# Delta rule in a two-block model: ScalarE scales the query-state product, VectorE adds the rest, and ScalarE sums the squares

## The reference, cut to what matters

```python
def step(state, inp):
    u_i, w_i, qg_i, kd_i, att_i, dl_i = inp
    v_new = u_i - jnp.einsum("bhcd,bhde->bhce", w_i, state)
    o = jnp.einsum("bhcd,bhde->bhce", qg_i, state) + jnp.einsum("bhij,bhje->bhie", att_i, v_new)
    state = state * dl_i[..., None, None] + jnp.einsum("bhcd,bhce->bhde", kd_i, v_new)
    return state, o
...
o_gdn = (rmsnorm_2(o_gdn, gdn_norm_g[l]) * jax.nn.silu(z))
```

## Time and profile before

| | us |
|---|---|
| median of 3 runs (2519.55 to 2521.11) | 2519.91 |
| the profiled execution | 2520.09 |
| its span, first to last instruction | 2518.3 |
| PE busy, 99% of the span | 2481.8 |
| DVE busy, 64% | 1619.7 |
| ACT busy, 48% | 1205.7 |

### The profile page before, as it was taken

The page is one execution under the profiler, slowest core; times in us unless marked ns, Lnnn a source line. Parts: engine busy times, 40 slices in busy tenths (PEclk is TensorE's granted clock), DMA queues, the critical chain, the costliest instruction groups (busy, mean ns, idle before and its releaser), DMA issues.

```text
span 2518.3 us, 37877 instructions
## 1 busy us (share of the span) xinstructions
PE 2481.8 (99%) x15440; PEld 2070.1 (82%) x15440; DVE 1619.7 (64%) x2585; ACT 1205.7 (48%) x2030; POOL 75.2 (3%) x114
## 2 busy tenths in 40 slices
PE   9999999999999999999999999999999999999998
PEld 7999888888877777878999888777776788888887
DVE  6888348866764554357887257766877655677733
ACT  6556244666555455245555246544333454444421
POOL 0111000000000000000110000000000000000000
PEclk9999999999999999999999999999999999999999
DMA  5776332222222222333775323211111112333232
GB/s 173 175 179 154 108 100 92 77 76 75 84 68 68 76 66 77 91 92 101 176 177 151 98 93 101 76 41 37 44 43 52 59 55 88 94 99 101 88 100 72
DMA packets 80525, 237.82 MB, mean 94 GB/s; under 512 B 8928, under 2 KB 10976, under 8 KB 80352
## 3 DMA queue, kind: packets, MB, share of 16 engines
q1 hardware_dynamic: 68832, 213.56, 27.0%
q0 software_dynamic: 10080, 18.35, 4.8%
q10 hardware_dynamic: 1440, 3.49, 0.4%
HBM read 233.27 MB, written 2.10 MB: 93 GB/s over the span
## 4 chain that ended last, share of the span: by engine, by line
PE 92%; DVE 5%; DMA 2%; ACT 1%; issue 1%; SPq 0%; ACTq 0%; DVEq 0%
PE bank L2208 22%; PE bank L2210 21%; PE bank L2209 21%; PE bank L2222 4%; PE bank L2224 4%; PE bank L2223 4%; PE bank L2441 2%; PE bank L2366 1%; PE bank L2280 1%; PE bank L2374 1%; DMA raw<-in_w2u 1%; PE bank L2360 1%; PE bank L2537 1%; PE bank L2347 1%; PE bank L2258 1%
## 5 line engine op out<-in xcount | busy, mean ns | idle before, releaser
L2208 PE MATMUL bank<-uR,hl 128*128 128x512 f32 x1684 | 685.4, 407 | 5.3 <-DVE uR L2954 2.8
L2943 DVE TENSOR_TENSOR hl<-raw,hl 128x1024 fp32r<-128x1024 f32 (+2 forms) x325 | 386.0, 1191 | 453.9 <-ACT hl L2586 452.8
L2210 PE MATMUL bank<-uR,hl 128*128 128x512 f32 x1684 | 658.3, 391 | 0.0
L2209 PE MATMUL bank<-uR,hl 128*128 128x512 f32 x1684 | 657.7, 391 | 0.0
L2586 ACT CAST hl<-raw 128x1024 fp32r<-128x1024 f32 (+2 forms) x325 | 329.8, 1020 | 207.2 <-PE bank L2210 196.1
L2208 PEld LDWEIGHTS bank<-uR,hl 128*128 128x128 f32 x1684 | 316.8, 188 | 94.8 <-issue 24.8
L2209 PEld LDWEIGHTS bank<-uR,hl 128*128 128x128 f32 x1684 | 317.1, 188 | 67.6 <-issue 7.2
L2210 PEld LDWEIGHTS bank<-uR,hl 128*128 128x128 f32 x1684 | 316.5, 188 | 67.7
L2937 DVE TENSOR_TENSOR hl<-raw,hl 128x1024 fp32r<-128x1024 f32 (+1 forms) x142 | 150.8, 1076 | 32.4 <-ACT hl L2582 29.4
L2222 PE MATMUL bank<-sum,hl 128*128 128x256 f32 x560 | 159.3, 284 | 2.5 <-DVE fA L3082 2.5
L2223 PE MATMUL bank<-sum,hl 128*128 128x256 f32 x560 | 158.7, 283 | 0.0
(11 more groups left out here) (499 smaller groups left out, 4385.5 us busy)
## 6 DMA issues: line engine op xcount, KB each, us to landing
raw<-in_win SPq DMA_DIRECT2D x147, 512.0 KB, 3.5
raw<-in_w SPq DMA_DIRECT2D x44, 512.0 KB, 3.5
raw<-in_w1u SPq DMA_DIRECT2D x54, 256.0 KB, 3.0
raw<-in_w2u SPq DMA_DIRECT2D x51, 256.0 KB, 3.1
raw<-in_w1g SPq DMA_DIRECT2D x22, 512.0 KB, 4.5
raw<-in_w2g SPq DMA_DIRECT2D x22, 512.0 KB, 4.3
raw<-in_w1d SPq DMA_DIRECT2D x16, 512.0 KB, 3.6
raw<-in_wssd SPq DMA_DIRECT2D x16, 512.0 KB, 3.5
```

The costliest lines, as they stand in the source:

```text
L2208: e.matmul(s.bank[:, :], h[:, 0, w], hi, start=s.first and q == 0, stop=False)
L2209: e.matmul(s.bank[:, :], h[:, 0, w], lo, start=False, stop=False)
L2210: i = e.matmul(s.bank[:, :], h[:, 1, w], hi, start=False, stop=s.last and q == n - 1)
L2943: e.tensor_tensor(h[:, 1, w], x[:, w], h[:, 0, w].bitcast(F), ALU.subtract).then_inc(*sig("dve_split.lo", s, i))
```

## The change

In `scan_s` ACT now writes `o`: it multiplies the query-state product by `exp(G)` out of PSUM (for chunk 0, where there is no state yet, it copies the attention product). DVE then makes one addition of the attention product to `o` where it made a copy and a multiply-add. In `gdn_norm` ACT squares `o` in eight pieces of 128 columns with the sum of each taken along; the two sums on DVE are gone. The planner's table gets the new figures, and because of them the plan between pair 0 and the sparse attention comes out in another order. The bank of the products is free after DVE's addition, as before.

```diff
@@ COSTS
-               ("DVE", 0.6, "dve_gdn.o")],
-    "gdn_norm": [("ACT", 1.25), ("DVE", 1.0, "dve_gdn.sum"), ("ACT Ln", 0.45), ("DVE", 1.4, "dve_gdn.on")],
+               ("ACT", 0.3, "act_gdn.o"), ("DVE", 0.3, "dve_gdn.o")],
+    "gdn_norm": [("ACT", 2.3, "act_gdn.sq", 1), ("ACT Ln", 0.45), ("DVE", 1.4, "dve_gdn.on")],
@@ scalar_program
+        def scan_s(s):
+            c, to = s.c, tcol(s.c % 4)
+            go.wait_ge(*on("pe_gdn.o", s))
+            go.wait_ge(*on("act_gdn.dl", s.cols))
+            if c % 4 == 0:
+                after(*s.o[c // 4].after)
+            if c:
+                x = e.mul(s.o[c // 4][:, to], s.bo[:, 0:128], of_pair(geg, s.p)[:, c, :])
+            else:
+                x = e.copy(s.o[0][:, to], s.bo[:, 128:256])
+            x.then_inc(*sig("act_gdn.o", s))
+
         def gdn_norm(s):
             rs = ors[:, 0:8]
             for n in range(2):
                 after(*s.o[n].t, *s.qs[n].after)
-                activate(s.qs[n][:, :], s.o[n][:, :], ACT.Square, scale=DSC).then_inc(*sig("act_gdn.sq", s, n))
-            go.wait_ge(*on("dve_gdn.sum", s))
+                for t in range(T4):
+                    x = activate(s.qs[n][:, tcol(t)], s.o[n][:, tcol(t)], ACT.Square, scale=DSC,
+                                 accum_out=rs[:, 4 * n + t:4 * n + t + 1])
+                x.then_inc(*sig("act_gdn.sq", s, n))
+            go.wait_ge(*on("act_gdn.sq", s, 1))
@@ vector_program
-            go.wait_ge(*on("pe_gdn.o", s))
-            if c % 4 == 0:
-                after(*s.o[c // 4].after)
             if c:
-                e.tensor_copy(s.o[c // 4][:, to], s.bo[:, 128:256]).then_inc(*sig("dve_gdn.o2", s))
-                go.wait_ge(*on("dve_gdn.o2", s))
-                x = e.scalar_tensor_tensor(out=s.o[c // 4][:, to], in0=s.bo[:, 0:128], scalar=of_pair(geg, s.p)[:, c, :],
-                                           in1=s.o[c // 4][:, to], op0=ALU.mult, op1=ALU.add)
-            else:
-                x = e.tensor_copy(s.o[0][:, to], s.bo[:, 128:256])
-            x.then_inc(*sig("dve_gdn.o", s))
+                go.wait_ge(*on("act_gdn.o", s))
+                e.tensor_tensor(s.o[c // 4][:, to], s.o[c // 4][:, to], s.bo[:, 128:256], ALU.add).then_inc(*sig("dve_gdn.o", s))
@@ vector_program gdn_norm
-            for n in range(2):
-                go.wait_ge(*on("act_gdn.sq", s, n))
-                x = e.reduce_sum(rs[:, 4 * n:4 * n + 4], v3(s.qs[n]), AX.X)
-            x.then_inc(*sig("dve_gdn.sum", s))
```

More of the change, by code:

```diff
@@ L1883, in gdn_scan @@
                 x.release(("dve_gdn.state", s2, i))
-            bo.release(("dve_gdn.o", s2))
+            bo.release(("dve_gdn.o" if c else "act_gdn.o", s2))
             before = s2
@@ L1897, in gdn_out @@
         for q in qs:
-            q.release(("dve_gdn.sum", s))
+            q.release(("act_gdn.sq", s, 1))
         yield from until(lambda: zg[hs[1]] is not None)
@@ L2902, in scalar_program @@
               "turn_v": turn_v, "pv_turn": pv_turn, "pv_mul": pv_mul, "att_front": att_front, "narrow": narrow,
-              "narrow_turn": narrow_turn, "gdn_decay": gdn_decay, "gdn_seed_turn": gdn_seed_turn, "gdn_level": gdn_level,
+              "narrow_turn": narrow_turn, "scan_s": scan_s, "gdn_decay": gdn_decay, "gdn_seed_turn": gdn_seed_turn, "gdn_level": gdn_level,
               "gdn_u": gdn_u, "gdn_w": gdn_w, "gdn_norm": gdn_norm, "ix_score": ix_score, "sp_front": sp_front}
```

## The result

The changed kernel takes 2523.09 us (median of 20 runs, 2520.08 to 2526.51) where the one before took 2519.60 on the same chip (20 runs, 2516.45 to 2521.79). The ratio is 1.0016, with a 95% interval of 1.0010 to 1.0023: 0.16% slower, inside the 0.2% that the prediction calls no change. The forecast was 2522.5 in 2514 to 2529. The profiled execution took 2521.15 us, its span is 2519.3.

A forecast was written before the change was run, and what follows sets the result against it. PE, busy 2481.8 of 2518.3 us, was taken as the bound, with waits and lost clock of about 16 us. Five terms (-3.6, +3.6, +1.6, -0.8, +1.8) sum to +2.6 us: 2522.5 from the median, range 2514 to 2529.

The forecast's parts named there:

- End of pair 3's scan: Panel steps break up the run of scan steps; waits of 1.0 and 1.9 and lost clock go, one 1.0 stays: -3.6 us.
- Seed of pair 1: PE waits 2.3 us for DVE's seed and 0.4 before `scan_s` 3, 0.8 is hidden, one clock drop 1.7: +3.6 us.
- Norm of pair 3: The copy `turn_v` needs stands behind the whole norm on ACT; PE waits 2.2 us, not 0.7: +1.6 us.
- Pair 3's dense stretch: The seed's wait and lost clock stay; added PE work cuts waits 2.7 us, `ix_mask` costs 1.9: -0.8 us.
- Pair 2: A convolution and searches stand on DVE ahead of the scan's subtraction in its dense stretch: 0 to 2.5, taken as +1.8 us.
- hidden wait: In `scan_s`, DVE's addition waits for ACT's product, hidden by the state updates: costed at nothing, 3 us if cover fails.
- its signs: L2450 and L2354 waits over 2 us; 1950 rows gone; clock 1.00 there, under 1 at 1700; DVE 16 us less; squares 0.40 apart.
- the 8 that would have told against the mechanism: Over PE's waits and lost clock: a change of their sum by more than 8 us would show the mechanism wrong.
- rival A: Freed DVE shortens PE's waits in the two stretches where DVE is over 90% busy: faster, about 2511.5 us, chance 0.15.
- B: Waits at pair 1's seed, `ix_mask` and pair 2's convolution each pull the clock to 1.2 GHz: slower, 2528 us, chance 0.28.
- C: Across the kernel, waits that go equal those that come, PE's work being fixed: same time, 2520 us, chance 0.07.

The follow-up runs named there:

- e1: The changed kernel's new arithmetic (both edits) in the order of steps of the kernel before; 2516.25 us, ratio 0.9986 to the kernel before.
- e2: The arithmetic of the kernel before in the changed kernel's order of steps; 2526.29 us, ratio 1.0026 to the kernel before.
- e5: The kernel before with only the new `scan_s`, old norm and old order kept; 2515.69 us, ratio 0.9990.
- e4: The changed kernel with `ix_mask` of row block 2 moved behind the last `scan_s` of pair 2; 2520.43 us, ratio 1.0000 to the kernel before.
- e12: The changed kernel with two panel steps ahead of each of the seeds of pairs 1 and 3 on PE; 2518.42 us, ratio 0.9996 to the kernel before.
- e9: e1 with panel steps brought forward on PE: two ahead of pair 3's seed, one each ahead of its `scan_v` 7 and `scan_s` 7; 2511.20 us.
- e8: e7 with pair 3's `scan_v` and `scan_s` of chunk 7, norm and `gdn_out` put later in the plan; 2513.28 us, ratio 0.9979 to the kernel before.
- e3: The changed kernel with DVE's seed of pairs 1 to 3 directly behind the scaling of the keys; 2522.90 us, ratio 1.0009 to the kernel before.
- e6: The kernel before with only the new norm (eight squares with sums), old `scan_s` and old order kept; 2519.48 us, ratio 1.0003.
- e11: The changed kernel with pair 3's norm behind the first `turn_v` and the last `gdn_out` behind the second; 2523.41 us, ratio 1.0018 to the kernel before.
- e7: e1 with two panel steps moved ahead of pair 3's seed on PE; 2513.08 us, ratio 0.9977 to the kernel before.

## Why the prediction was right

The sum of +2.6 us holds: +3.5 between the medians (interval of the ratio: 2.5 to 5.8 us), +2.6 in the two traces between a wait of PE at about 1489 us, ahead of all that was changed, and the second `turn_v`. Ahead of 1489 us the changed kernel's trace is 1.5 us the shorter one, though nothing was changed there; two single executions can be compared only with that margin. The terms, with the prediction's price of the clock (half of the time at the low level, 1.7 us for each 3.41 us):

1. **End of pair 3's scan, forecast -3.6.** The waits of 1.03 and 1.86 and a lost 1.7 became one wait of 0.94: -3.7. The order alone would have done it, and partly the arithmetic alone too: e1, in the old order, keeps 0.94 and 1.48 and loses the clock drop. The prediction had credited this to the order only.

2. **Seed of pair 1, forecast +3.6.** The wait is 2.33 us, the forecast 2.3, and the clock lost 1.7. The 0.4 ahead of `scan_s` 3 did not come. With the small waits around it: +3.1.

3. **Norm of pair 3, forecast +1.6.** `turn_v` waited 1.57 us and not 2.2: +0.9. The mis-sized number is the square with its sum. ACT's timeline of the changed kernel:

```profile
1970.76 0.29 ACT L2563 ACTIVATE fA<-fB 128x128 f32<-128x128 f32 x1
1970.95 0.19 ACT L2563 ACTIVATION_READ_ACCUMULATOR fA<-fB 128x1 f32 x1
1971.05 0.29 ACT L2563 ACTIVATE fA<-fB 128x128 f32<-128x128 f32 x1
...
1972.92 1.28 ACT L2561 ACT_TABLE_LOAD   x1
1974.21 0.55 ACT L2563 ACTIVATE small<-small 128x8 f32<-128x8 f32 x2
1974.66 0.57 ACT L2788 COPY fB<-bank 128x512 f32<-128x512 f32 x1
```

The squares stand 1971.05 - 1970.76 = 0.29 us apart, not 0.40: the read of the sum (0.19 us) overlaps the end of its own square and the start of the next, and the row that the 0.40 was taken from the earlier trace rows has a column operand. Eight take 2.4 us, 0.8 less than the 3.2 of the sum. The Trainium skill's figure ("VectorE: DVE Perf Modes", the errata section, 224 cycles and one for each element at 1.2 GHz) gave 2.35 us, an estimate that this trace agrees with, and with it the place would have been put at +0.8. And e2 has a wait of 1.4 us there with the old squares and sums, so most of the 1.6 comes from where the norm stands. (The forecast of this term also took 1.44 us for two panel pieces, where the earlier trace rows has 1.47; that is 0.1 us.)

4. **Pair 3's dense stretch, forecast -0.8.** `ix_mask` cost more, 2.59 us against 1.9, and the waits in this stretch rose from 5.3 to 5.7. What made it -1.3 was the clock: 3.41 us at the low level where before had 6.83, behind the same wait of 2.00. That was not foreseen, and it is no doing of the change that can be shown (last section). It is also priced too high: e5 has 6.83 us at the low level here and e1 has 3.41, in the same order and with the same scan, and from the seed to the next indexer step PE needs 40.52 us in e5 and 39.58 in e1, 0.9 more. With 0.9 for the step the term is -0.5.

5. **Pair 2, forecast +1.8.** From 0.5 to 2.6 us of waits, +2.1: 0.55, 0.57, 0.32 and 1.12, the last being the scan's subtraction behind the convolution, as said.

Sum of the five as measured: -3.7 + 3.1 + 0.9 - 1.3 + 2.1 = +1.1 us, or +1.9 with -0.5 for the fourth. The traces have 2.6 between the same two points; 0.7 to 1.5 us are open. So every term has the right sign and lies within 0.7 us of its forecast, which is the merit of the prediction; that the total came out within 1 us is in part luck, since the open part and errors of both signs went into it, and one execution differs from the next by as much.

**The hidden wait** held: of its 28 times DVE's addition waited once for ACT's product, 0.4 us at 1726 us, and PE has no wait behind it:

```profile
L3466 DVE TENSOR_TENSOR fA<-fA,bank 128x128 f32<-128x128 f32 x14 | 3.9, 279 | 0.4 <-ACT fA L2879 0.4
L3466 DVE TENSOR_TENSOR fB<-fB,bank 128x128 f32<-128x128 f32 x14 | 3.9, 280 | 0.0
```

**Of its signs**, these came: L2450 waits over 2 us twice (2.33 and 2.00), the row L2509 for DVE at 1950 is gone and one wait of 0.94 at L2491 is left, the clock is 1.00 there and falls at about 1703, and DVE has 16 us less. Two did not: the longest wait of L2354 is 1.57 and not over 2, and the squares are not 0.40 apart. PE's waits and the lost clock together changed by +2.7 - 1.7 = +1.0 us, far from the 8 that would have told against the mechanism.

**What the prediction lacked** is the arithmetic as a term of its own. It worked place by place on the whole change and named DVE's relief only as rival A, with 0.15. A's mechanism is real: with the order held, the arithmetic gains 3.5 us. A's time of 2511.5, some 8 us below before, is wrong twice over: the arithmetic gains less than half of that, and the new order takes twice what it gains. B's mechanism showed in part: the clock did fall at pair 1's seed, for the shorter stretch in the changed kernel's trace and for B's 6.83 us in those of e2 and e4, and not at pair 2 or at `ix_mask`, unless the seeds were covered (e12). C's equality of what goes and what comes is the nearest of the three in size, but the two sides are an order that costs and arithmetic that pays, not the same waits elsewhere. Had the terms been split, the forecast would also have said what to do: keep the arithmetic, refuse the order.

## What to carry to other kernels

When an edit changes the work and, through a planner's figures, the order, run the work in the old order and the old work in the new one: here 2.5 to 3.5 us of gain and 6.6 to 7.6 us of loss hid behind 0.16%. Where the bounding engine waits some 2 us for a chain on another engine, put work of its own that waits for nothing ahead of the wait, and leave the other engine's order alone: in e9 the covered waits went and none came, in e8 and e3 the moved steps of DVE made new ones. A shorter instruction on an engine that is 64% busy is worth only what its neighbours at PE's waits gain from it: 16 us less on DVE gave about 3.

## What the runs showed of the hardware

The low clock does not hold equally long behind the same wait. Behind pair 3's seed, with a wait of 2.00 us, the 1.2 GHz level lasted 6.83 us in before, e5 and e6, 3.41 us in the changed kernel, e1, e4 and e11, and in e2 the clock did not fall there at all. Behind pair 1's seed, with 2.33 us in the same order of instructions, it lasted 3.41 us in the changed kernel and e11 but 6.83 in e4. A wait of 2.59 us had no drop behind it in the changed kernel and one of 3.41 us in e12, whose panel steps had removed the two drops ahead of it; why, the runs do not say.

Nor does a drop cost what its length says. Half of 3.41 us would be 1.7. Here are the changed kernel and then e4, with the same order of instructions from pair 1's seed to a later step of PE:

```profile
1702.51 1.33 PE L2450 MATMUL bank<-con,gx 64*64 64x64 f32 x32 [2.33 <-DVE gx L3416]
...
1747.56 1.98 PE L2280 MATMUL bank<-fB,onesc 128*128 128x512 f32 x4 [0.55 <-DVE fA L3462]
```

```profile
1704.01 1.97 PE L2459 MATMUL bank<-con,gx 64*64 64x64 f32 x32 [2.33 <-DVE gx L3425]
...
1749.94 1.98 PE L2289 MATMUL bank<-fB,onesc 128*128 128x512 f32 x4 [0.55 <-DVE fA L3471]
```

That is 45.05 and 45.93 us: the second 3.41 us at the low level cost 0.9. At 1130 us, in code that no edit touches, a drop cost nothing. The changed kernel has one there and the kernel before has none, behind the same waits of PE (0.47, 0.5 and 0.6). The stretch and PE's next long wait, changed kernel first, then before:

```profile
1130.00:1133.20 3.20, 3.20 (x16) 3.20 (x16) 3.17 (x7) 1.82 (x3) 0.00 (x0) 0.50 0.01 3
1134.72 0.38 PE L2261 MATMUL bank<-uR,hl 128*128 128x256 f32 x1 [0.83 <-DVE uR L3012]
```

```profile
1130.00:1133.20 3.20, 2.77 (x21) 2.36 (x19) 3.17 (x7) 1.92 (x4) 0.00 (x0) 1.00 0.01 3
1134.81 0.38 PE L2261 MATMUL bank<-uR,hl 128*128 128x256 f32 x1 [1.65 <-DVE uR L2997]
```

From the matmul that waited 0.47 us to this one it is 7.8 us in both, and so in all 14 traces, with the drop or without: what PE lost to the clock it did not have to wait for DVE. The drop at 1130 us is in 7 of the 14 traces (the changed kernel, e1, e3, e4, e7, e9, e12). So half of the low stretch is an upper bound of what it costs; a single trace must be read with that margin, and the times of many runs are the better measure.
